# Later chunks' pair searches at the head of the next batch's front, in a hybrid decoder block with expert retrieval

## What is computed

```
for each chunk of 128 tokens (8 of them), xn = rmsnorm(x2):
    q  = xn @ wq                      # 8 heads x 2 halves of 128
    s1, s2 = scores of both halves against 128 keys each
    v1, i1 = top16(s1);  v2, i2 = top16(s2)
    cand = v1[:, None] + v2[None, :]  # 256 pairs a head
    best, pos = top16(cand)           # "pair search"
    idx = i1*128 + i2 at pos          # 16 experts a head, 128 a token
    g   = softmax(best)
    w   = g * gelu(xn . u_tab[idx])
    x2 += sum over 128 experts of w * v_tab[idx]
y = rmsnorm(x2)
```

## Time and profile before

| | |
|---|---|
| median of 3 runs | 3487.49 us |
| the profiled execution, its own time | 3493.22 us |
| its span | 3491.5 us |
| PE busy | 2454.5 us (70%) |
| DVE busy | 2663.4 us (76%) |
| ACT busy | 687.7 us (20%) |
| POOL busy | 1382.3 us (40%) |
| DMA | 347 GB/s over the span; 1073.81 of 1212.83 MB are the gathers |
| chain that ended last | PE 34%, DVE 29%, DMA 23%, ACT 6%, issue 5% |

### The profile page before, as it was taken

The page is one execution under the profiler, slowest core; times in us unless marked ns, Lnnn a source line. Parts: engine busy times, 40 slices in busy tenths (PEclk is TensorE's granted clock), DMA queues, the critical chain, the costliest instruction groups (busy, mean ns, idle before and its releaser), DMA issues.

```text
span 3491.5 us, 29071 instructions
## 1 busy us (share of the span) xinstructions
PE 2454.5 (70%) x7552; PEld 1321.4 (38%) x7552; DVE 2663.4 (76%) x6520; ACT 687.7 (20%) x1947; POOL 1382.3 (40%) x1296
## 2 busy tenths in 40 slices
PE   8569895589989785675878787576667555554554
PEld 7447463246545342223544333243223222211221
DVE  1674689865778799897779788689877577777776
ACT  2122311121434111112114332111111111111111
POOL 0132323333334333444445445344444344444442
PEclk9779998899999897887889899898788777777777
DMA  6878697789888998889999999999888899999997
GB/s 217 313 299 325 266 381 292 292 334 356 331 330 329 380 355 311 325 339 368 415 411 377 341 370 388 387 394 371 334 356 340 337 374 380 380 370 372 380 383 293
DMA packets 185037, 1212.83 MB, mean 347 GB/s; under 512 B 20672, under 2 KB 20672, under 8 KB 53440
## 3 DMA queue, kind: packets, MB, share of 16 engines
q0 software_dynamic: 147456, 1073.81, 78.7%
q1 hardware_dynamic: 37440, 137.40, 10.4%
HBM read 1198.54 MB, written 12.58 MB: 347 GB/s over the span
## 4 chain that ended last, share of the span: by engine, by line
PE 34%; DVE 29%; DMA 23%; ACT 6%; issue 5%; POOL 2%; POOLq 0%; DVEq 0%; ACTq 0%; SPq 0%
DMA ring<-in_uv,cur_idx 22%; PE vacc L900 17%; DVE ring L1075 11%; PE bank L938 6%; DVE acc L1106 4%; ACT diag L731 3%; PE bank L1006 3%; PE o_ps L904 2%; POOL ring L694 2%; DMA xn<-in_final_norm_g 1%; PE bank L934 1%; DVE lt L1223 1%; DVE ocT L1233 1%; PE bank L949 1%; PE bank L967 1%
## 5 line engine op out<-in xcount | busy, mean ns | idle before, releaser
L900 PE MATMUL vacc<-ring,diag 128*128 128x512 f32 x2048 | 1267.1, 763 | 985.5 <-ACT diag L731 983.2
L694 POOL DMA_INDIRECT ring<-in_uv,cur_idx x1024 | 1215.1, 1187 | 1172.5 <-PE vacc L900 611.6
L1075 DVE CUSTOM_DVE_ANT_0 ring<-ring,xn 128x1024 f32<-128x1024 f32 x1024 | 1219.5, 1222 | 351.6 <-DMA ring<-in_uv,cur_idx 349.0
L900 PEld LDWEIGHTS vacc<-ring,diag 128*128 128x128 f32 x2048 | 481.7, 246 | 1670.2 <-ACT diag L731 1027.2
L1106 DVE SCALAR_TENSOR_TENSOR acc<-ring,g_w,acc 128x512 f32<-128x512 f32 x832 | 625.6, 752 | 35.2 <-DVE g_w L1098 0.6
L685 POOL COPY cur_idx<-idx 128x4 uint32<-128x4 uint32 (+1 forms) x256 | 165.2, 645 | 904.9 <-DVE acc L1106 693.6
L726 ACT ACTIVATE g_ex<-g_cu 128x4 f32<-128x4 f32 x256 | 52.4, 205 | 2071.6 <-DVE g_cu L1088 2055.3
L731 ACT ACTIVATE diag<-ident,g_w 128x128 f32<-128x128 f32 x1024 | 326.8, 390 | 187.8 <-DVE g_w L1098 184.5
L938 PE MATMUL bank<-hT,wpool 128*128 128x256 f32 (+2 forms) x1280 | 285.0, 382 | 1.4 <-ACT hT L757 1.4
L938 PEld LDWEIGHTS bank<-hT,wpool 128*128 128x128 f32 x1280 | 219.8, 192 | 69.1 <-issue 12.1
L1017 PE MATMUL bank<-hT,wpool 128*128 128x256 f32 (+2 forms) x1024 | 235.9, 386 | 0.7 <-ACT hT L839 0.7
(11 more groups left out here) (126 smaller groups left out, 1798.2 us busy)
## 6 DMA issues: line engine op xcount, KB each, us to landing
wpool<-in_w_in SPq DMA_DIRECT2D x96, 512.0 KB
wpool<-in_peer_wq SPq DMA_DIRECT2D x64, 512.0 KB
wpool<-in_w_out SPq DMA_DIRECT2D x32, 512.0 KB
ring<-in_uv,cur_idx POOLq DMA_INDIRECT x1024
xb<-in_x SPq DMA_DIRECT2D x15, 512.0 KB
x_scratch<-xb SPq DMA_DIRECT2D x8, 512.0 KB
xn_scratch<-xb SPq DMA_DIRECT2D x8, 512.0 KB
xn<-xn_scratch SPq DMA_DIRECT2D x8, 512.0 KB
```

The lines of the kernel that those rows point to most:

```text
L694: nc.gpsimd.indirect_dma_start(ring[:, s, :], None, uv, bass.IndirectOffsetOnAxis(ap=cur_idx[:, s:s + 1], axis=0))\
L900: ins = nc.tensor.matmul(vacc[:, :], diag[:, q, s, :], ring[:, q * GROUP + s, D:D + PE_COLS], start=first and s == 0, stop=last and s == G ...
L1075: ins = nc.vector.tensor_tensor_reduce(out=ring[:, s, 0:D], in0=ring[:, s, 0:D], in1=xn[:, c % 2, :], scale=1.0, scalar=0.0, op0=ALU.mult, ...
```

## The change

Batches 1 and 2 keep in their own fronts only the pair searches of their first chunk. The searches of chunk 2 stand at the head of the steps of stage 2, and those of chunks 4 and 5 at the head of the steps of stage 3. The last batch keeps all its searches. The number of steps is the same.

```diff
     if bi > 0:
         k += 4
-        for c in chunks:
+        for c in chunks if bi == len(BATCHES) - 1 else chunks[:1]:
             for h in range(0, PH, hs):
                 search(at, k, c, h)
                 k += 4
     return [steps[i] for i in sorted(steps)]
+def late_steps(bi):
+    steps = {}
+    def at(k, eng, *phase):
+        steps.setdefault(k, []).append((eng, *phase))
+    if 0 < bi < len(BATCHES) - 1:
+        k = 0
+        for c in BATCHES[bi][1:]:
+            for h in range(0, PH, heads_per_search(bi)):
                 search(at, k, c, h)
                 k += 4
     return [steps[i] for i in sorted(steps)]
...
-    steps = {bi: front_steps(bi) for bi in range(1, len(BATCHES))}
+    steps = {bi: late_steps(bi - 1) + front_steps(bi) for bi in range(1, len(BATCHES))}
```

More of the change, by code:

```diff
@@ L158, in front_steps @@
         k += 4
-        for c in chunks:
+        for c in chunks if bi == len(BATCHES) - 1 else chunks[:1]:
             for h in range(0, PH, hs):
+                search(at, k, c, h)
+                k += 4
+    return [steps[i] for i in sorted(steps)]
+def late_steps(bi):
[6 more added lines that the diff above has]
+            for h in range(0, PH, heads_per_search(bi)):
                 search(at, k, c, h)
```

## The result

The changed kernel takes 3515.76 us (median of 5 runs, 3512.69 to 3523.49) against 3490.67 us of the kernel before (5 runs, 3483.1 to 3493.02). The ratio is 1.0073, 95% interval 1.0048 to 1.0099: slower by 25 us, where 19 us faster was forecast, and 10 us above the top of the range. The profiled executions differ by 3512.69 - 3493.22 = 19.5 us; stage by stage that is the difference to explain.

A forecast was written before the change was run, and what follows sets the result against it. PE was taken to bound projections and attention, DVE queries and searches, in stages 1 and 2, and mostly gathers stage 3. Terms -36 - 30 + 47 = -19 us gave 3474 us profiled, 3468 against the median; range 3430 to 3506.

The forecast's parts named there:

- Attention by PE: Groups added beside attention in stages 1 and 2 were priced at PE's matmul time, 3.94 us each.
- Stage 1: Chunk 0: the searches of chunk 2 leave, their groups go elsewhere; forecast -36 us, ends -24 and -45.
- Stage 2: Chunks 1 and 2: four searches leave, two arrive at the head; forecast -30 us, between -53 and -7.
- The late stretch: Head of stage 2: two searches of chunk 2 beside 6.3 ordinary groups, at DVE's plain sum, 91.4 us.
- The stall on the final gain: Stage 2: DVE's 18.39 us wait behind weight loads goes, a burst costing 11.6 us stays; booked -7 us.
- Stage 3: Chunks 3 to 5: four searches arrive beside 18.7 ordinary groups; forecast +47 us, between +12 and +83.
- The wide groups: 20 groups stop being wide, each then needing 3.12 us of row adds on DVE; 62 us more DVE work.
- The issue delay: POOL might issue 80 gathers of newly ordinary groups 0.186 us later each: 15 us, total -4 us; mostly slack expected.
- (d): Rival, chance 0.10: stages 1 and 2 give little, groups beside projections and attention cost DVE's 9.04 us; +16, 3504 us.
- (a): Rival, chance 0.13: gathers hold all of stage 3 and hide the late searches; stage 3 +12, total -54, 3433 us.
- (b): Rival, chance 0.17: stage 3 gives all back, at +62 to +65; total about -3, 3484 us.
- (c): Rival, chance 0.05: stage 3's front, squeezed into fewer groups, becomes the slower bound; 65 us more, total +46, 3533 us.

## Why the prediction was wrong, point by point

**The bounds.** Projections by PE and the searches by DVE: right in the main; relieving the named engine took 15 of 24 us off the projections of stage 2 and 14 of some 20 off its late searches. Queries of stage 2 by DVE: right only as far as DVE is the first of several, since without 14 groups' row adds (14 x 3.12 = 44 us) they fell by 13 us. Attention by PE: wrong, and this is the step that failed. It was "PE is nearest, so I take PE's price" in stage 1, and in stage 2 the same from a busy share of 252/274. There a group costs about 10.5 and 7.5 us, not 3.94. For 1.3 and 1.7 groups that is 9 and 6 us of the error. What sets the price stays open. It is no one engine's time for a group: relieving DVE, PE or the gathers alone took 1 to 6 us off 308, two of them 17 to 21, all three 41.5.

**Stage 1: -25 instead of -36.** Attention +14.9 for 5.2 booked (the price above); queries +14.5 for 9.0: DVE's price was too low where the DMA share is 0.98; a group's gathers at that stretch's 393 GB/s take 11.3 x 372/393 = 10.7 us, and the other 4 us stay unexplained. Searches +7.2 for 4.1 (the moved searches took 59.2 us by interpolation, and the row fell by 52.0): the added 0.7 group there is ordinary, since wide groups start at the next whole group. The end that I gave, -24, was what happened, though 3 of the 25 us were gained ahead of group 5.3, where both kernels have the same order: that part is the scatter of one execution.

**Stage 2: -4 instead of -30.** The late stretch took 98 us for 91: DVE was busy 87 of 92 us in it, so the sum was nearly right and the chunk's boundary came on top. Attention and queries together took 30.5 us more where I had booked 11.6; that is 19 of the 26 us of error. The stall on the final gain did go: the changed kernel's `final_scale` of chunk 1 has no wait before it (timeline of DVE; before: the earlier trace rows).

```profile
1136.47 1.27 DVE L1349 SCALAR_TENSOR_TENSOR acc<-acc,st,xn 128x1024 f32<-128x1024 f32 x1
```

And the burst of weight tiles came, at group 74, as had been booked: dot products wait for gathers four times.

```profile
1260.35 1.22 DVE L1091 CUSTOM_DVE_ANT_0 ring<-ring,xn 128x1024 f32<-128x1024 f32 x1 [4.14 <-DMA ring<-in_uv,cur_idx]
1264.12 1.23 DVE L1091 CUSTOM_DVE_ANT_0 ring<-ring,xn 128x1024 f32<-128x1024 f32 x1 [2.53 <-DMA ring<-in_uv,cur_idx]
1267.91 1.22 DVE L1091 CUSTOM_DVE_ANT_0 ring<-ring,xn 128x1024 f32<-128x1024 f32 x1 [1.36 <-DMA ring<-in_uv,cur_idx]
1271.71 1.22 DVE L1091 CUSTOM_DVE_ANT_0 ring<-ring,xn 128x1024 f32<-128x1024 f32 x1 [2.57 <-DMA ring<-in_uv,cur_idx]
```

By these waits 18.4 us went and 10.6 came, -8 for the -7 booked. In the table this is hidden: attention before holds about 10 us of the stall and after 10.6 of the burst, so that its row shows nothing of it, and the queries' row has the other 8 or 9 us of the gain. So the 1.7 groups beside attention cost some 21 us for the 6.6 booked, and the 1.3 beside the queries some 17 or 18 for 12.0. Of the 14 us missed beside attention 6 are the group's price by the line above (7.5 us), and 8 stand above that line; which alignment of steps makes them, no run settles. They are no accident of one execution: the kernel with wide groups beside the late searches, which has the same order, took 311 us there.

**Stage 3: +46 for +47.** Each term came out within 8 us: its rows had the bound that the prices assumed, and the attention's price was taken between two engines' and not at the lowest.

**The wide groups** were in the sum, as dearer groups where they were moved to, and the counts were right. But the sum never stated them as a term. Stated alone they are worth 39 us, twice the gain forecast, and the sign hung on whether the freed stages would take ordinary groups cheaply.

**The issue delay** did not come: POOL's mean issue is 1187 ns before and 1182 after, although 80 more row adds stand on DVE. Groups by line, whole span, before and after:

```profile
L694 POOL DMA_INDIRECT ring<-in_uv,cur_idx x1024 | 1215.1, 1187 | 1172.5 <-PE vacc L900 611.6 <-PE o_ps L904 221.3 <-issue 205.1
```
```profile
L710 POOL DMA_INDIRECT ring<-in_uv,cur_idx x1024 | 1210.1, 1182 | 1125.4 <-PE vacc L916 674.6 <-issue 210.6 <-PE o_ps L920 133.1
```

The late stretch of stage 3 shows the same with one thing changed: 1194 ns with the row adds (1559 to 1800 us), 1183 ns with these groups wide (1547 to 1785 us in that run). So the difference of 1302 and 1116 ns in the earlier trace rows belongs to the stretches and not to the row adds.

**The rivals.** (d), stages 1 and 2 give little, came nearest (3504 us); it had 0.10. Its condition, DVE's price for every group beside projections and attention, is in effect what happened beside attention, though not by DVE; projections kept PE's price (+2.4 and +6.2 us for 3.9 and 5.2 booked). (a), (b) and (c) all changed stage 3, which was right. The range let stages 1 and 2 miss by 10 and 23 us as if independent; both rested on one price and missed together, by 11 and 26.

## What to carry to other kernels

A busy share of 0.92 on one engine does not make its time the price of more work there: look at the next engine's share too (DVE 0.83, DMA 0.85 here), and vary the amount of work in a run before trusting a price. Here a group cost 7.5 to 10.5 us over the whole range, where PE needs 3.94, DVE 9.04 and the gathers 11.3. When an interpolated table is read, see first whether a long stall lies on the border of two rows. When work is moved between stages, move it only to where another resource clearly holds the pace, one move at a time: of two moves in one edit, one gained 10 us and the other lost 22. And count what an edit's side effect (here 20 wide groups) costs as a term of its own.

## What the runs showed of the hardware

In one run relief of PE came back in part as a lower clock. With half of PE's slots left out, stage 2's attention has PE's granted clock at 0.85 instead of 0.92, and the matmuls left take longer: 763 ns instead of 675 (window of this run; groups by line, the changed kernel and then this run).

```profile
929.00:1234.00 305.00, 242.76 (x882) 133.23 (x883) 245.72 (x491) 119.56 (x269) 124.53 (x111) 0.85 0.87 337
```
```profile
L916 PE MATMUL vacc<-ring,diag 128*128 128x512 f32 x177 | 93.3, 675 | 35.8 <-ACT diag L747 35.8
```
```profile
L918 PE MATMUL vacc<-ring,diag 128*128 128x512 f32 x92 | 57.8, 763 | 37.4 <-ACT diag L747 37.4
```

93.3 - 57.8 = 35.5 us of these matmuls went, while PE's whole busy time fell by 19. Attention's own matmuls, of which none was left out, show it too: the 60 of them that multiply by `neg_tri` went from 592 to 653 ns each. The Trainium skill, "TensorE: Matmul & The Clock Gate", Part 1, says that the clock has two levels, 1.2 and 2.4 GHz, and that sustained activity is what gives the higher. The trace agrees in that the stretch's mean lies between the two and is lower in this run, where PE is busy 243 of 305 us instead of 262 of 308. PE's busy share alone does not give the clock: in the run that leaves out the adds besides, PE is busy the same 0.80 of the stretch, 229 of 287 us, and the clock is 0.90.
